# The first stage of a two-layer block on one core: condition weights by pairs of tiles, and the first four fills tile by tile

## The reference

```python
cond = silu(c)
mod = cond @ w_ada + b_ada                     # 1024 -> 6 x 1024
sh1, sc1, g1, sh2, sc2, g2 = split(mod, 6)
u = layer_norm(h) * (1.0 + sc1) + sh1          # h = x: 512 positions x 1024 features
z = u @ w_in                                   # the first products
```

## Time and profile before

| | us |
|---|---|
| three runs | 2946.81, 2947.54, 2949.56 |
| median | 2947.54 |
| span of the profiled execution, first to last instruction | 2947.4 |
| TensorE busy in it | 2914.6 (99%) |
| first product of fill 0 | 39.65 |
| fill 3 done, fill 4 begins | 62.9 |

### The profile page before, as it was taken

How to read it: one execution, slowest core, us unless ns; L and a number is a source line. 1 busy time by engine, 2 the same in 40 slices (tenths; PEclk the granted TensorE clock), 3 DMA queues, 4 the chain that set the end, 5 groups by cost and what they waited for, 6 DMA issues and landing times.

```text
span 2947.4 us, 52217 instructions
## 1 busy us (share of the span) xinstructions
PE 2914.6 (99%) x20726; PEld 2340.7 (79%) x20726; DVE 1289.6 (44%) x1814; ACT 1093.7 (37%) x1536; POOL 1474.3 (50%) x1824
## 2 busy tenths in 40 slices
PE   9999999999999999999999999999999999999999
PEld 5887778878888777777778888887777777888887
DVE  5827742381111658433657222225944365732210
ACT  4455653352222443224553322224322445432322
POOL 4643345545555556224337555665622433755555
PEclk9999999999999999999999999999999999999999
DMA  7731132313233233226343222333322633432233
GB/s 265 277 102 51 51 99 87 99 52 107 94 99 106 86 109 125 70 75 222 101 160 116 95 94 99 103 105 117 119 71 81 212 110 129 142 99 94 98 101 127
DMA packets 104761, 335.21 MB, mean 114 GB/s; under 512 B 10608, under 2 KB 11024, under 8 KB 103824
## 3 DMA queue, kind: packets, MB, share of 16 engines
q1 hardware_dynamic: 77648, 277.06, 28.6%
q10 hardware_dynamic: 26944, 55.67, 5.1%
HBM read 303.84 MB, written 28.84 MB: 113 GB/s over the span
## 4 chain that ended last, share of the span: by engine, by line
PE 79%; issue 8%; POOL 6%; DVE 4%; ACT 1%; DVEq 1%; DMA 1%; ACTq 0%; POOLq 0%; SPq 0%
PE psum L405 68%; POOL w_lo L376 6%; PE psum L795 5%; DVEq L1720 1%; DMA arena<-scratch 1%; DVE XL L1723 1%; PE psum L1046 0%; PE psum L1026 0%; PE psum L534 0%; PE psum L1040 0%; PE psum L544 0%; PE psum L1062 0%; DVE arena L1741 0%; PE psum L734 0%; PE psum L982 0%
## 5 line engine op out<-in xcount | busy, mean ns | idle before, releaser
L376 POOL TENSOR_TENSOR w_lo<-w_raw,w_hi 128x256 fp32r<-128x256 f32 x1820 | 1474.1, 841 | 1468.4 <-ACT w_hi L1098 1320.1
L405 PE MATMUL psum<-XH,w_hi 128*128 128x512 f32 x2592 | 1047.1, 404 | 10.7 <-DVE arena L1969 3.5
L405 PE MATMUL psum<-XL,w_hi 128*128 128x512 f32 x2592 | 1012.5, 391 | 0.0
L405 PE MATMUL psum<-XH,w_lo 128*128 128x512 f32 x2592 | 1012.4, 391 | 0.0
L1098 ACT ACTIVATE w_hi<-w_raw 128x1024 fp32r<-128x1024 f32 x436 | 460.4, 1056 | 685.0 <-PE psum L405 580.6
L405 PEld LDWEIGHTS psum<-XH,w_hi 128*128 128x128 f32 x2592 | 487.4, 188 | 135.9 <-issue 19.4
L405 PEld LDWEIGHTS psum<-XL,w_hi 128*128 128x128 f32 x2592 | 487.5, 188 | 104.2
L405 PEld LDWEIGHTS psum<-XH,w_lo 128*128 128x128 f32 x2592 | 487.9, 188 | 101.2 <-issue 7.7
L405 PE MATMUL psum<-HH,w_hi 128*128 128x512 f32 x976 | 383.0, 392 | 3.4 <-DVE arena L2354 3.4
L405 PE MATMUL psum<-HL,w_hi 128*128 128x512 f32 x976 | 379.9, 389 | 0.0
L405 PE MATMUL psum<-HH,w_lo 128*128 128x512 f32 x976 | 379.8, 389 | 0.0
(11 more groups left out here) (345 smaller groups left out, 2368.0 us busy)
## 6 DMA issues: line engine op xcount, KB each, us to landing
w_raw<-in_fills SPq DMA_DIRECT2D x456, 512.0 KB, 3.3
scratch<-arena ACTq DMA_DIRECT2D x86, 256.0 KB, 2.1
arena<-in_fills SPq DMA_DIRECT2D x32, 512.0 KB, 4.2
arena<-scratch ACTq DMA_DIRECT2D x10, 1024.0 KB, 7.7
arena<-in_w_ada SPq DMA_DIRECT2D x4, 2048.0 KB, 19.6
H<-scratch ACTq DMA_DIRECT2D x4, 2048.0 KB, 11.5
scratch<-H SPq DMA_DIRECT2D x2, 2048.0 KB, 8.1
arena<-scratch SPq DMA_DIRECT2D x32, 128.0 KB, 3.8
```

What stands on the lines that cost most here:

```text
L376: ins = nc.gpsimd.tensor_tensor(w_lo[:, to:to + FILL // 4], w_raw[:, of:of + FILL // 4], w_hi[:, to:to + FILL // 4].bitcast(F32), ALU.subt ...
L405: ins = mm(out_ap, wt[:, w:w + 128], xt[:, x0:x0 + T], start=first and k == 0 and o == 0, stop=last and k == n - 1 and o == 2)
```

## The change

- **Condition weights.** The 8 MB come in pairs: piece k holds the shift weights of tiles 2k and 2k + 1 and the scale weights of the same tiles, in two DMAs of 1 MB. Piece 0 is ahead of fills 0 and 1, piece 1 behind them, then fill 2 and piece 2, fill 3 and piece 3, each behind one more `lo_ready`. The four later chunks are started ahead of fill 6 and not of fill 4.
- **Sums.** The sums of `x` and of the squares are made with 32 columns of ones, tile t in column group t mod 4 (`grouped_sums`); VectorE copies the four partial sums out of PSUM (`groups_out`), and one product with the 128 x 128 ones adds them up (`total`). All 32 rows of a group are equal, hence the further factor 1/32.
- **Normalising.** VectorE applies scale and shift of two tiles at a time, as their columns come.
- **Low parts.** Those of fills 0 to 3 move from GpSimd to VectorE, as one instruction of 128 x 1024 each (`first_low`).
- **First products.** Fills 0 to 3 go tile by tile as `first_part`, with rows and columns 1 to 3 of the condition among them. Some `idle_products` go.

The diff, cut to its core:

```diff
+            def ada_piece(k):
+                for half in range(2):
+                    of = dram["w_ada"][2 * half + k // 2][:, k % 2 * 8 * KB:(k % 2 + 1) * 8 * KB]
+                    sp.dma_start(A(40 + 16 * k + 8 * half, 8 * KB), of).then_inc(sem(f"ada_in{k}"), 16)
+            ada_piece(0)
+            first_fill(0)
+            first_fill(1)
+            ada_piece(1)
+            for f in (2, 3):
+                sp.wait_ge(lo_ready, f - 1)
+                first_fill(f)
+                ada_piece(f)
...
-                if n == 4:
+                if n == 6:
                     sp.wait_ge(sem("ada_done"), 4)
...
-            for f in range(3):
-                lo_part(f, f)
-            lo_parts(3, FILLS_1 + LAYERS * FILLS_L)
+            lo_parts(4, FILLS - 8)
+            for k in range(3):
+                lo_part(FILLS - 4 + k, k)
...
+            def grouped_sums(b, tile, ready):
+                for t in range(DT):
+                    if t % 2 == 0:
+                        ready(t // 2)
+                    g = 32 * (t % 4)
+                    ins = mm(bank(b)[g:g + 32], C("ones", 32), tile(t), start=t < 4, stop=t >= 4)
+                ins.then_inc(sem("ln_sum"), 1)
+            def total(b, n, done):
+                pe.wait_ge(sem("ln_groups"), n)
+                mm(bank(b), C("ones", 128), A(GROUPS_KB), start=True, stop=True).then_inc(sem(done), 1)
...
             condition_rows(0)
-            squares_sum(0)
+            grouped_sums(2, lambda t: A(16, T, t * T), lambda q: pe.wait_ge(sem("ln_sq"), q + 1))
+            total(3, 2, "ln_var")
+            condition_columns(0)
+            idle_products(2, 2)
             condition_rows(1)
-            condition_columns(0)
-            condition_rows(2)
-            condition_columns(1)
-            idle_products(2, 4)
+            for k in range(4):
+                for f in range(2):
+                    first_part(f, k)
+                if k == 0:
+                    condition_columns(1)
+            for f in range(2, 4):
+                for k in range(4):
+                    first_part(f, k)
+                if f == 2:
+                    condition_rows(2)
+            condition_columns(2)
+            for f in range(2):
+                first_part(f, 4)
             condition_rows(3)
-            condition_columns(2)
-            idle_products(1, 4)
+            for f in range(2, 4):
+                first_part(f, 4)
             condition_columns(3)
-            idle_products(3, 4)
-            first_two(0, 0, 0, lambda t: pe.wait_ge(sem("ln_x"), t + 1))
-            next_two(0, 0, 0)
+            for f in range(4):
+                first_part(f, 5)
+            for f in range(4):
+                for k in (6, 7):
+                    first_part(f, k)
...
-            for k in range(1, 4):
-                rows_out(k)
-            for t in range(DT):
-                first_x(t)
-                if t == 1:
+            for k in range(4):
+                if k == 2:
                     first_hi(2)
-            first_hi(3)
+                    first_hi(3)
+                if k:
+                    rows_out(k)
+                first_x(2 * k)
+                first_x(2 * k + 1)
...
+            def first_low(f):
+                dve.wait_ge(hi_ready, f + 1)
+                to, of = slice(f * FILL, (f + 1) * FILL), slice(f % 2 * FILL, (f % 2 + 1) * FILL)
+                lo(w_lo[:, to], w_raw[:, of], w_hi[:, to]).then_inc(lo_ready, 1)
```

More of the change, by code:

```diff
@@ L300, in ada_chunk @@
                     .then_inc(sem(f"ada_in{a % 4}"), 16)
-            for n in range(2, FILLS_HG + 4 * HEADS // 2 + 2):
+            for n in range(4, FILLS_HG + 4 * HEADS // 2 + 2):
                 a = 2 * (n - 6 - ADA_FILL) + 4
-                if n == 4:
+                if n == 6:
                     sp.wait_ge(sem("ada_done"), 4)
@@ L540, in _ @@
             idle_products(3, 3)
-            for t in range(DT):
-                if t % 2 == 0:
-                    pe.wait_ge(x_in[t // 2], 16)
-                ins = mm(bank(4), C("ones", 128), H[:, t * T:(t + 1) * T], start=t == 0, stop=t == DT - 1)
-            ins.then_inc(sem("ln_sum"), 1)
+            grouped_sums(0, lambda t: H[:, t * T:(t + 1) * T], lambda q: pe.wait_ge(x_in[q], 16))
+            idle_products(1, 3)
+            total(1, 1, "ln_sum")
+            idle_products(2, 3)
             def condition_rows(k):
-                pe.wait_ge(sem(f"ada_in{k}"), 16)
+                pe.wait_ge(sem(f"ada_in{k}"), 32)
                 w = A(40 + 16 * k, 16 * KB).rearrange("p (t k c) -> p t k c", k=DT, c=128)
@@ L1207, in _ @@
             rows_out(0)
-            for f in range(2):
-                first_hi(f)
-            ln_rstd(0, RSTD_KB)
+            first_hi(0)
+            ln_rstd(0, RSTD_KB, 3, 1.0 / D / 32)
+            first_hi(1)
             def first_x(t):
@@ L1727, in all_out, with groups_out, centred @@
                     dve.wait_ge(chunk_out[b], c)
-            def centred(n, mean):
-                dve.wait_ge(sem("ln_sum"), mean)
+            def groups_out(n, b):
+                dve.wait_ge(sem("ln_sum"), n)
+                cp(A(GROUPS_KB), bank(b)).then_inc(sem("ln_groups"), 1)
+            def centred():
+                dve.wait_ge(sem("ln_sum"), 2)
                 for q in range(4):
-                    stt(chunks(A(0, 2 * T, 2 * q * T), T), bc(bank(4), 2), -1.0 / D, chunks(Ht(2 * q, 2), T), ALU.mult, ALU.add)\
+                    stt(chunks(A(0, 2 * T, 2 * q * T), T), bc(bank(1), 2), -1.0 / D / 32, chunks(Ht(2 * q, 2), T), ALU.mult, ALU.add)\
                         .then_inc(sem("ln_xc"), 1)
@@ L2014, in _ @@
                 drain()
[L2015 removed]
+            ins.then_inc(sem("ln_groups"), 1)
             head_low(HEADS - 1)
[L2018 removed]
+            dve.wait_ge(sem("ln_sum"), 4)
             for q in range(4):
```

83 lines of the change are left out of this document (46 added, 37 removed).

## The result

On one chip, runs of both kernels taken in turn: the kernel before has a median of 2948.98 us (six runs, 2946.81 to 2950.58), the changed kernel one of 2961.56 (six runs, 2953.95 to 2967.62). The ratio is 1.0036, with a 95% interval of 1.0022 to 1.0050: slower by 10.6 us (6.5 to 14.7). The prediction said 2955.0, range 2946 to 2960, with half of the chance on slower. The direction was right; the forecast was 7.6 us over the kernel before. The range was counted from a median of 2947.54 for that kernel: from there 10.6 us more is 2958.1, within it, while the median of these runs, in which the kernel before takes 2948.98, is 1.6 us beyond it.

The account below looks back on a forecast made before the run. TensorE, busy 99%, was taken to bound the kernel, through when fill 4 begins. Fill 3's end 0, wait at fill 4 3.3, clock falls 2.0 and 2.3 sum to 7.6 over 2947.4: 2955.0 us, range 2946 to 2960.

Parts of the forecast that it names:

- The opening: Up to the first product: quicker sums give 1/std at 23.65, 5.2 earlier, and the first product 10.3 earlier, at 29.35.
- The early start is spent again: First product to fill 3's end: the 10.3 and 1.4 gained go on insertions and waits; fill 3 ends at 62.9 as before.
- insertions: Two rows at 2.3 and three columns at 1.05 inside TensorE's stream of the first fills: 7.7 us.
- waits inside the stream: TensorE waits 1.6 ahead of tile 2 and 2.4 ahead of tile 4: 4.0 us.
- the first two falls: Clock falls at the first product and tile 4: 2.0 for the first, the second left out of the sum.
- the wait at fill 4: TensorE waits 3.3 us for fill 4's low part, with ends of 2.0 and 4.5.
- I count two falls: Clock halves behind the waits at the first product and at fill 4, costing 2.0 and 2.3 us.
- the case that the prediction held at 0.15: Rival: the clock falls three times, also at tile 4 for 1.7; 9.3 us slower, 2956.7; chance 0.15.
- a slower TensorE fills the very waits that slow it: Argument for the rival that the clock falls once or not at all: 3.3 to 5.3 slower, about 2951.8; chance 0.20.
- The rival of the early start: Waits for tiles 2 and 4 vanish, fill 3 ends at 58.9, 1 to 4 us gained, about 2945.5; chance 0.17.
- fill 4 at 57.0 or earlier: What over 0.2% faster would need, with the waits gone and fill 4's low part early; chance 0.04.
- that rival: Small column groups do not pay in the opening sums: 10 to 13 us slower, about 2959; chance 0.14.

Follow-up runs that it names:

- e3_opening: Kernel before with only the small column groups for the sums of x and of the squares; median 2950.46 us, ratio 0.9998 to the kernel before.
- e8_first: Changed kernel with 8 idle products ahead of the first product only; median 2959.30 us, ratio 1.0027 to the kernel before.
- e1_idle: Changed kernel with idle products in three TensorE waits (first product, tile 4, fill 4); median 2955.26 us, ratio 1.0016 to the kernel before.
- e2_consts: Changed kernel with ScalarE's two constants DMAs started behind the high part of fill 1; median 2956.59 us, ratio 1.0020 to the kernel before.
- e5_both: Changed kernel with early constants and idle products ahead of the first product and tile 4; median 2952.44 us, ratio 1.0007 to the kernel before.
- e4_gpsimd: Changed kernel with the low parts of fills 0 to 3 back on GpSimd; median 2959.93 us, ratio 1.0032 to the kernel before.
- e9_columns: Changed kernel with condition weights ahead of fills 2 and 3, rows and columns 1 to 3 ahead of tile 3; median 2951.77 us, ratio 0.9999 to kernel before.
- e6_reorder: Changed kernel, columns early, fills 0 and 1 finished first, fills 2 and 3 low parts on GpSimd, early constants, idle products; 2943.50 us, ratio 0.9971 to kernel before.
- e7_order: Changed kernel with early constants, two idle sets, tiles 5 to 7 of fills 0 and 1 first; 2952.42 us, ratio 1.0004 to kernel before.

## Why the prediction was right in direction and short in size

- **The opening.** Sums ready and copied at 12.11 (12.0 in the working), subtraction from 14.02 (13.75), 1/std at 24.20 (23.65), first product 29.84 (29.35), wait 3.48 (3.4). Each link within 0.55 us. That the quick sums alone give the first product only 0.6, since it hangs on the last piece of the weights there, is shown by `e3_opening`.
- **The early start is spent again.** Shown. The working had fill 4 at 62.9 + 2.0 + 3.3 = 68.2; it started at 72.79. The 4.6 between them, term by term from the rows above: first product +0.5; insertions 6.4 and not 7.7 (two rows of 1.94, three columns of 0.8 to 0.95), -1.3; waits inside the stream 2.52 and not 4.0, -1.5; the first two falls 6.2 and not 2.0, +4.2; the wait at fill 4 5.46 and not 3.3, +2.2; and +0.5 for the product behind each insertion and wait, which takes 0.1 longer to the next. The third and the fourth of these belong together: 1.2 of the first fall's 4.5 is time in which TensorE would have waited for tile 2 (`e8_first`).
- **The insertions** were overpriced. Rows 2 begin 0.09 behind the last product's usual distance of 0.23 and take 1.94 of the stream, not 2.3. The 0.76 of the earlier trace rows did not come back (0.35 here, behind products in the faster format), and with it goes the rule of the Trainium skill, "TensorEngine Tiling (Array Packing)", Key Properties, that was weighed: no drain of the engine is to be seen at this change of mode. The first 32-column pass starts at 43.38, 0.32 behind the start of the last product.
- **The step that failed is "I count two falls".** There are three: the case that the prediction held at 0.15. The one at tile 4 was left out of the sum, though its wait was forecast (2.4, measured 2.52); it costs 1.7, the size given for it. The first was mis-sized: 4.5 and not 2.0, since it lasted 10.2 us with TensorE busy for 8.9 of it, where the stretches of the earlier trace rows have 3.4 and 6.8. `e1_idle` and `e8_first` show that the clock is the cause: with TensorE kept busy ahead of the first product, fill 5 comes 3.6 earlier; in all three waits, 6.5 (3.0 and 6.1 counted from the first product). As to the Trainium skill's "TensorE: Matmul & The Clock Gate", the section on HAM oscillation, which would have each short burst between waits start low, the trace agrees for the three long waits here, where the stretch at 0.50 was 10.2, 3.4 and 6.8 us long. It does not agree with "every time": the waits of 2.38 (`e2_consts`) and 2.40 (`e5_both`) at fill 4 had no fall. Nor was a count from the earlier trace rows as firm as it looked. In the same trace another wait had no fall:

```profile
328.30 0.50 PE L405 MATMUL psum<-XH,w_hi 128*128 128x512 f32 x1 [1.75 <-DVE arena L1969]
```

- **The rival** "a slower TensorE fills the very waits that slow it" was right for tile 2, whose 1.6 disappeared, and nowhere else.
- **Fill 4.** The mechanism was right in each part (all four fills end together, table, copy, high part, GpSimd, constants late), the constants' landing was mis-sized: 6.6 from issue where the earlier trace rows has 4.2, with an issue of 1.30 for 0.45. The upper bound of 4.5 for the wait was too low by 1.0. `e2_consts` shows their price: 3.1 of wait, and there the fall with it. That the landing is slow because of the 2 MB of later chunks issued at 56.76, 4 us before the constants, was not tried by itself, but the traces fit it: in the five with the chunks issued 4 to 5 us before (the changed kernel, `e1_idle`, `e4_gpsimd`, `e8_first`, `e9_columns`) `par` lands 6.0 to 7.6 behind its issue, in the three where they were issued 12 us before (the kernel before, `e3_opening`) or after it (`e6_reorder`), 4.2 to 4.3. (With the early constants, among the condition weights, it is 10.7 to 11.2.)
- **The rival of the early start** fell for this kernel and for the reason given, columns 2 behind 15 us of work. It was right as a mechanism: `e9_columns` takes the columns ahead and is level with the kernel before in its runs (2.5 later at fill 5), `e6_reorder` also ends fills 0 and 1 first and gains 8.6 us. The prediction's "fill 4 at 57.0 or earlier" for a gain beyond 0.2% was about the right mark: it came at 57.52. The 5.2 us at fill 5 lie a little below the 8.6 (5.6 to 11.5) of its runs; where the rest comes from is open.
- **The small groups pay** in the changed kernel: 1/std comes 4.7 earlier, and that rival fell. In the old order of the weights they bring 2.0 of it (`e3_opening`).

What stays open: why the clock came back only after 10.2 us in the first fall and after 3.4 in the second; why a wait of the same length has a fall in one trace and none in another; and what sets the two late waits.

## What to carry to other kernels

An early start is worth what the last thing of the stage gets of it: look at the wait that ends the stage, here fill 4's, and follow its inputs back, before counting what is gained in front. Work that feeds a chain on other engines (here the columns, 1 us of TensorE, with 3.5 us of VectorE and ScalarE behind them) belongs as early as its data allow, and of several results the one whose buffer is needed next should be finished first, not all of them together (`e6_reorder` does both; the order alone, in `e7_order`, brought nothing while the columns were late). Where a stream begins earlier than its inputs can follow, new waits open inside it. Here the three of 2.5 to 5.5 us were each paid twice, once as a wait and once as a stretch at half the clock; a few idle products in the wait took away the second price.

## What the runs showed of the hardware

- Idle products of 256 columns in waits of 2.5 to 5.5 us kept the granted clock at 1.00 (`e1_idle`, `e5_both`, `e7_order`), and the remaining gaps of 0.25 to 2.4 had no fall behind them. Without idle products the waits of 3.5 to 3.9 ahead of the first product and of 2.5 at tile 4 had a fall in each of the four traces that have them, those of 4.8 to 5.5 at fill 4 in each of three. A gap of 2.34 at fill 4 had one (`e9_columns`), gaps of 2.38 and 2.40 had none (`e2_consts`, `e5_both`); one of 1.75 had one at 287 in the kernel before and one of 1.75 at 328 none; the wait of 3.26 for fill weights had one at 414 in the kernel before and none at 426 in `e4_gpsimd`. So the length of the gap does not decide by itself.
- The fall around the first product lasted 10.2 us in the changed kernel and in `e4_gpsimd`, where it began 1.3 to 1.5 us ahead of that product, and 6.8 in `e2_consts` and `e9_columns`, where it began 0.8 to 0.9 behind it.
- VectorE's instructions take longer beside GpSimd's subtractions on 128 x 256 tiles: two `TENSOR_SCALAR` of 128 x 512 1.73 for 1.00, a `TENSOR_TENSOR` of 128 x 1024 1.74 for 1.22 (`e4_gpsimd` against the changed kernel). GpSimd's four took 3.23 there and 2.77 to 2.80 at other times (20.96 and 37.67).
- Sixteen passes of 32 columns in four column groups cost 1.94 of a running stream of 128-column products, 0.09 of it at the entry; at 0.50 they take 3.64 (`e9_columns`).
- A 68 KB DMA landed 4.2 to 4.3 us behind its issue in three traces, and 6.0 to 7.6 in the five in which 2 MB on another queue had been issued 4 to 5 us before it.
